# A second buffer for the conditioning sums of a two-layer streaming encoder, with their transposes and VectorE's collection of them at later steps

## The chip, the cores and the metric

The kernel runs on one core of one Trainium2 chip. The metric is device time in microseconds, the median over several executions.

## What is computed

Two layers of an encoder are run for 320 tokens (256 of a prompt, 64 of running streams) of width 1024, all in 32-bit floats. Each layer takes a conditioning vector per token group and turns it into nine vectors of 1024 (a shift, a scale and a gate for each of three parts of the layer); the parts are a feed-forward, a token mixer (retention and differential attention) and a second feed-forward:

```python
mod = (jax.nn.silu(c) @ w_ada[l] + b_ada[l]).reshape(B, N_SUB, 3, D_MODEL)[:, :, :, None, :]
x = x + 0.5 * mod[:, 0, 2] * _swiglu(pre(x, 0), w_ff_up[l, 0], w_ff_down[l, 0])
mix, k_new, v_new, s_new = _token_mix(pre(x, 1), pos, lambda_init, w_in[l], w_out[l], ...)
x = x + mod[:, 1, 2] * mix
x = x + 0.5 * mod[:, 2, 2] * _swiglu(pre(x, 2), w_ff_up[l, 1], w_ff_down[l, 1])
```

Here pre(t, i) is the root-mean-square norm with the i-th scale and shift. The matrix w_ada of a layer is 1024 by 9216; the product with it is what the change is about.

## The kernel before, in words

**Steps.** A layer is 76 steps, each with its own piece of weights: 22 up steps of the first feed-forward (one block of 128 of the 2816 hidden columns, gate and value halves), 8 down steps, 12 of the input projection, 4 of the output projection, and again 22 up and 8 down steps. A step is numbered s in its layer; within a feed-forward f, i counts up steps 0 to 21 and m down steps 0 to 7, and the prediction counts the down steps on as 22 to 29. SyncE (SP) loads a step's weights into one of two buffers (raw, L368 to L379), two steps ahead. ScalarE (ACT) rounds them to a high part (w_hi, its split, L909), VectorE (DVE) and, for a part of the columns, GpSimd (POOL) subtract that from the weights to get the low part (w_lo, L1126 and L1564). TensorE (PE) then multiplies in three passes, high by high, low by high and high by low (L513 to L515): 48 matmuls in an up step, 66 in a down step, each in two halves. Before each half it waits for the half's low part (half_ready, L517). The split of step s + 2 on ScalarE waits for the end of step s on TensorE (step_done), since both use one buffer.

**Around a step on VectorE.** In its instruction order (ffn, L1214) step i is: units of the conditioning sums (ada_unit, L1129), then for an up step the product of gate and value (gate_up, L1188, which waits for ScalarE's silu of the step), for a down step the update of x (down_evac, L1207, which waits for the step's end), then the split of step i + 2.

**The conditioning sums.** w_ada is cut into blocks of 512 columns, 18 to a layer. The first layer's blocks 0 to 5 are made ahead of the loop over layers; the rest, and the next layer's first six, are spread over the feed-forwards by a plan written by hand (ada_plan, L300). It gives (block, place) pairs, where a place counts the blocks in the order in which a layer makes them. A block is four units; SyncE brings a unit (512 KB) to one of four buffers ada_raw behind the weights of a step (load_ada, L393), once VectorE has used that buffer. A unit is four instructions of 128x512 on VectorE (L1137, L1139): each row of the unit times its value of silu(c), for two token groups, added to the sums ada_acc. In the up steps there is one unit in each step and a block takes four steps; from up step 20 on there are two units in each step and a block takes two. In the first feed-forward sums are made in all 30 steps, the last of them after the norm that follows; in the first layer's second feed-forward in steps 0 to 25, in the second layer's in steps 0 to 7.

**Turn and reduction.** ada_acc then holds a partial sum for each of 128 partitions. When the fourth unit is done VectorE drains and says acc_ready (L1144). TensorE transposes the eight 128x128 pieces into two banks of PSUM (turn_acc, L528; the transposes are L533), between the two halves of a step: of the step after the block's last unit (4, 8, 12, 16, 20, and then the down steps 22, 24, 26, 28). VectorE waits for acc_turned and reduces each bank over the partitions into mod (ada_reduce, L1148; L1151), two instructions, right behind the split at the end of the block's last step, so that the wait is for the turn in the step that TensorE does next. The next block's first unit follows and overwrites ada_acc. Place 9 is turned in the second step of the input projection (L835). finish_mod (L1154) adds the bias and the ones when a part's blocks are there.

**Loops.** VectorE and SyncE run the up steps in loops of four steps and down steps 0 to 3 in a loop of two; TensorE has a loop over up steps 12 to 19. Semaphore values and column indices in them are worked out from the loop's register. All engines run the two layers in a loop too. ScalarE and POOL have loops of their own.

Of the kernel before, what the change touches and what calls it, by code (L numbers as in the profile page):

```python
# [19 lines left out]
F32 = mybir.dt.float32  # L20
# [5 lines left out]
P = 128  # L26
# [3 lines left out]
DEPTH = 2  # L30
# [96 lines left out]
def encoder(nc, x_prompt, x_sample, cache_k, cache_v, state_ret, c_prompt, c_sample, w_ada, b_ada, g_norm,  # L127
# [18 lines left out]
    with ExitStack() as ctx:  # L146
# [45 lines left out]
        ada_acc = nc.alloc_sbuf_tensor_at("ada_acc", [P, 2, 512], F32, offset=after_g + 4 * 4096)  # L192
# [47 lines left out]
        acc_turned = sem("acc_turned")  # L240
        first_landed = [sem(f"first_landed{s}") for s in range(2)]
# [118 lines left out]
        def _(sp):  # L360
# [39 lines left out]
            def load_ffn(l, f, s0):  # L400

                bodies, last_up, downs = ada_plan(f)
                for (b, place), n0, n in ((bodies[0], 0, 2), (bodies[1], 2, 3)):
                    with sp.Fori(0, n) as j:
                        for v in range(4):
                            load_up(l, f, s0 + 2 + 4 * n0 + v, 2 + 4 * n0 + v + 4 * j, 2 * j)
                            with if_next(sp, l, b):
                                load_ada(l, b, place, v, j)

                def next_layer(v):  # L410
                    with sp.If(l < DEPTH - 1):
                        load(l, STEPS + v, 0, up_parts(DEPTH - 1, 0, v))

                def pair(block, load_next):
                    for v in range(2):
                        load_next(v)
                        if block:
                            with if_next(sp, l, block[0]):
                                load_ada(l, *block, 2 * v)
                                load_ada(l, *block, 2 * v + 1)  # L420

                pair(last_up, lambda v: load_down(l, f, s0 + UP + v, v, 0))
                with sp.Fori(0, 2) as j:
                    for v in range(2):
                        load_down(l, f, s0 + UP + 2 + v, 2 + v + 2 * j, j)
                        with if_next(sp, l, downs[0][0]):
                            load_ada(l, *downs[0], 2 * v, j)
                            load_ada(l, *downs[0], 2 * v + 1, j)
# [1242 lines left out]
```

## Time and profile before

| | |
|---|---|
| time, median of 3 | 1645.44 us (1642.21 to 1646.52) |
| profiled execution | span 1643.2 us from its first to its last instruction; no other time of it is given |
| granted TensorE clock, mean | 0.937 of full speed |
| TensorE / VectorE / ScalarE / POOL busy | 1469.8 / 1202.0 / 606.7 / 502.7 us |
| read from memory | 255 MB, 159 GB/s over the span |

Busy time counts an engine's instructions without waits, branches and semaphores. In the rows, "idle before" is how long the engine stood still just before an instruction, and the arrow names what ended that; DVEq is VectorE's sequencer, and "issue" is time in which the engine waited for nothing that the profile shows. Times in rows of a timeline are microseconds from the start of the span.

### The profile page before, as it was taken

Reading aid. Unit: us, or ns where it says so; the run is one execution under the profiler, and the core shown is the slowest. Engines: PE = TensorE matmul, PEld = TensorE weight load, DVE = VectorE, ACT = ScalarE, POOL = GpSimd, SP = SyncE. Lnnn points to the kernel's source line nnn. Section 1 sums busy time; section 2 is a strip of 40 time slices with the busy share of each in tenths; the row PEclk is TensorE's granted clock in tenths of the full one; section 3 lists DMA queues with packets and bytes.
Section 4 is the critical chain, followed back from the end, with each engine's and each line's share of the span. In section 5 each row is a group of like instructions: output and inputs, shape, how many; then the busy total and the mean of one; then the engine's idle time right before and its main releaser. Section 6 shows DMA issues by size and latency. Waiting matters only on the chain.

```text
span 1643.2 us, 27178 instructions
## 1 busy us (share of the span) xinstructions
PE 1469.8 (89%) x8865; PEld 1319.9 (80%) x8865; DVE 1202.0 (73%) x1697; ACT 606.7 (37%) x999; POOL 502.7 (31%) x343
## 2 busy tenths in 40 slices
PE   6889998889986889998898999889899769999998
PEld 2589988867763879998887999888677448899998
DVE  3988899987555488889948888998764546874552
ACT  2344432223434344443223444322234333444522
POOL 1134343314001133334323434432330102343432
PEclk9999999999985899999998999989999669999999
DMA  9657777533520147678643777865242204565652
GB/s 311 197 174 211 230 225 217 174 108 124 175 91 7 55 131 214 194 215 231 183 138 95 210 212 213 241 184 188 103 160 92 72 1 129 146 179 145 174 147 63
DMA packets 340962, 261.20 MB, mean 159 GB/s; under 512 B 7968, under 2 KB 288112, under 8 KB 340720
## 3 DMA queue, kind: packets, MB, share of 16 engines
q1 hardware_dynamic: 339456, 255.25, 51.6%
q0 software_dynamic: 1392, 4.46, 0.9%
q8 instruction: 69, 1.13, 0.3%
q14 instruction: 45, 0.37, 0.1%
HBM read 255.22 MB, written 4.46 MB: 158 GB/s over the span
## 4 chain that ended last, share of the span: by engine, by line
PE 47%; DVE 21%; DVEq 13%; DMA 7%; issue 6%; ACT 4%; SPq 1%; ACTq 0%; POOL 0%
PE ps L513 10%; PE ps L514 10%; PE ps L515 10%; DVE ada_acc L1139 9%; DMA ada_raw<-in_w_ada 6%; DVEq L1142 5%; DVEq L1144 4%; PE ps L672 4%; PE ps L677 4%; PE ps L673 4%; DVE w_lo L1126 3%; DVE f_buf L1182 2%; PE ps L533 1%; PE ps L812 1%; DMA first_ada<-in_w_ada 1%
## 5 line engine op out<-in xcount | busy, mean ns | idle before, releaser
L1126 DVE TENSOR_TENSOR w_lo<-raw,w_hi 128x1024 fp32r<-128x1024 f32 (+3 forms) x304 | 429.8, 1455 | 109.5 <-ACT w_hi L909 83.8
L513 PE MATMUL ps<-h_hi,w_hi 128*128 128x320 f32 x1408 | 441.2, 313 | 13.0 <-DVE w_lo L1126 10.3
L514 PE MATMUL ps<-h_lo,w_hi 128*128 128x320 f32 x1408 | 438.3, 311 | 0.0
L515 PE MATMUL ps<-h_hi,w_lo 128*128 128x320 f32 x1408 | 438.3, 311 | 0.0
L909 ACT ACTIVATE w_hi<-raw 128x1024 fp32r<-128x1024 f32 (+1 forms) x304 | 324.9, 1119 | 281.2 <-PE ps L515 188.4
L1139 DVE SCALAR_TENSOR_TENSOR ada_acc<-ada_raw,silu_c,ada_acc 128x512 f32<-128x512 f32 x448 | 391.3, 914 | 34.9 <-DMA ada_raw<-in_w_ada 22.3
L1564 POOL TENSOR_TENSOR w_lo<-raw,w_hi 128x512 fp32r<-128x512 f32 (+1 forms) x112 | 225.1, 2010 | 464.1 <-ACT w_hi L909 464.1
L513 PEld LDWEIGHTS ps<-h_hi,w_hi 128*128 128x128 f32 x1408 | 267.5, 190 | 16.2 <-DVE w_lo L1126 12.9
L514 PEld LDWEIGHTS ps<-h_lo,w_hi 128*128 128x128 f32 x1408 | 267.3, 190 | 0.0
L515 PEld LDWEIGHTS ps<-h_hi,w_lo 128*128 128x128 f32 x1408 | 267.2, 190 | 0.0
L513 PE MATMUL ps<-g_hi,w_hi 128*128 128x320 f32 x704 | 227.3, 323 | 13.4 <-DVE w_lo L1126 13.2
L514 PE MATMUL ps<-g_lo,w_hi 128*128 128x320 f32 x704 | 224.8, 319 | 0.0
L515 PE MATMUL ps<-g_hi,w_lo 128*128 128x320 f32 x704 | 224.4, 319 | 0.0
L513 PEld LDWEIGHTS ps<-g_hi,w_hi 128*128 128x128 f32 x704 | 139.2, 198 | 15.2 <-issue 13.7
L1569 POOL TENSOR_TENSOR g_lo<-f_buf,g_hi 128x320 f32 (+1 forms) x88 | 125.1, 1422 | 81.9 <-ACT g_hi L939 81.9
L514 PEld LDWEIGHTS ps<-g_lo,w_hi 128*128 128x128 f32 x704 | 139.2, 198 | 0.0
L515 PEld LDWEIGHTS ps<-g_hi,w_lo 128*128 128x128 f32 x704 | 138.8, 197 | 0.0
L672 PE MATMUL ps<-w_hi,h_hi 128*128 128x512 f32 (+1 forms) x288 | 118.2, 410 | 4.8 <-ACT h_hi L934 4.8
L1598 POOL TENSOR_TENSOR small<-small,minus_half 128x8 f32<-128x8 f32 (+3 forms) x24 | 31.7, 1325 | 281.3 <-DVE small L1272 281.3
L673 PE MATMUL ps<-w_lo,h_hi 128*128 128x512 f32 (+1 forms) x288 | 113.8, 395 | 0.0
L950 ACT ACT_TABLE_LOAD x40 | 51.3, 1283 | 120.5 <-PE ps L515 115.7
L1555 POOL TENSOR_TENSOR h_lo<-f_buf,h_hi 128x320 fp32r<-128x320 f32 x48 | 43.9, 915 | 162.6 <-ACT h_hi L934 162.6
(156 smaller groups left out, 1602.5 us busy)
## 6 DMA issues: line engine op xcount, KB each, us to landing
raw<-in_w_ff_up SPq DMA_DIRECT2D x176, 512.0 KB, 5.0
ada_raw<-in_w_ada SPq DMA_DIRECT2D x128, 512.0 KB, 6.1
raw<-in_w_ff_down SPq DMA_DIRECT2D x64, 704.0 KB, 6.1
raw<-in_w_in SPq DMA_DIRECT2D x48, 512.0 KB, 4.6
first_ada<-in_w_ada SPq DMA_DIRECT2D x8, 1024.0 KB, 7.1
raw<-in_w_out SPq DMA_DIRECT2D x16, 512.0 KB, 5.5
out<-arena POOLq DMA_DIRECT2D x9, 256.0 KB, 4.1
arena<-in_cache_k SPq DMA_DIRECT2D x2, 1024.0 KB, 5.5
```

What stands on the lines that cost most here:

```text
L513: pe.matmul(out, hi, mhi, start=start, stop=False)
L514: pe.matmul(out, hi, mlo, start=False, stop=False)
L515: return pe.matmul(out, lo, mhi, start=False, stop=stop)
L672: pe.matmul(out, h_hi[:, k, tok], wh, start=(k == 0), stop=False)
L673: pe.matmul(out, h_hi[:, k, tok], wl, start=False, stop=False)
L677: mm = pe.matmul(out, h_lo[:, k, tok], wh, start=False, stop=(k == KB - 1))
L909: act.activation(w_hi[s % 2][:, hf * w:(hf + 1) * w], raw[s % 2][:, hf * w:(hf + 1) * w], ACT.Copy).then_inc(hi_ready, 1)
L1126: dve.tensor_tensor(w_lo[s % 2][:, cols], raw[s % 2][:, cols], w_hi[s % 2][:, cols], ALU.subtract)\
L1139: last = dve.scalar_tensor_tensor(ada_acc[:, g, :], ada_raw[u][:, kk, :], c, ada_acc[:, g, :], ALU.mult, ALU.add)
L1142: dve.drain()
L1564: pool.tensor_tensor(w_lo[s % 2][:, cols], raw[s % 2][:, cols], w_hi[s % 2][:, cols], ALU.subtract)\
L1569: pool.tensor_tensor(block_of(g_lo, i + 2 * j), f_buf[:, i % 2, :], block_of(g_hi, i + 2 * j), ALU.subtract)\
```

## The change

The sums have two buffers, used in turn by even and odd places; the second lies where first_rows is, which is used before the loop over layers alone. The hand-written plan is replaced by a list of blocks with their first step and number of steps. The transposes of a block come in step first + n + 1, one step later on TensorE than before (5, 9, 13, 17, 21 and then 23, 25, 27, 29), and its reduction behind the split in the same step on VectorE, two steps later in VectorE's order than before. A semaphore mod_read, raised by the reduction, is waited for before the next block is turned, since the two PSUM banks are still one set. finish_mod(64, 72) moves from after up step 7 to after up step 10. Units, transfers and what they wait for are in the same steps as before. Loops over steps are written out on SyncE, TensorE and VectorE; place 9 is turned and reduced where it was.

```diff
-        ada_acc = nc.alloc_sbuf_tensor_at("ada_acc", [P, 2, 512], F32, offset=after_g + 4 * 4096)
+        ada_acc = [nc.alloc_sbuf_tensor_at(f"ada_acc{s}", [P, 2, 512], F32, offset=after_g + (4 + s) * 4096) for s in range(2)]
...
+        mod_read = sem("mod_read")
...
-        def ada_plan(f):
+        def ada_blocks(f):
             if f == 0:
-                return [(6, 0), (8, 2)], (11, 5), [(12, 6), (13, 7), (14, 8), (15, 9)]
-            return [(16, 10), (0, 12)], (3, 15), [(4, 16), (5, 17), None, None]
+                return [(6 + p, p, 4 * p, 4) for p in range(5)] + [(11 + p, 5 + p, UP - 2 + 2 * p, 2) for p in range(5)]
+            return [(16, 10, 0, 4), (17, 11, 4, 4), (0, 12, 8, 4), (1, 13, 12, 4), (2, 14, 16, 4),
+                    (3, 15, 20, 2), (4, 16, 22, 2), (5, 17, 24, 2)]
+
+        def units_in(f, step):
+            for b, place, first, n in ada_blocks(f):
+                if first <= step < first + n:
+                    each = 4 // n
+                    return b, place, range(each * (step - first), each * (step - first + 1))
+            return None
+
+        def turned_in(f, step):
+            for b, place, first, n in ada_blocks(f):
+                if first + n + 1 == step:
+                    return b, place
+            return None
+
+        def acc_of(place):
+            return ada_acc[place % 2 if place >= 0 else 0]
...
+                for q in range(2, UP + DOWN + 2):
+                    if q < UP:
+                        load_up(l, f, s0 + q, q, 0)
+                    elif q < UP + DOWN:
+                        load_down(l, f, s0 + q, q - UP, 0)
+                    elif f == 0:
+                        load_in(l, q - UP - DOWN)
+                    else:
+                        with sp.If(l < DEPTH - 1):
+                            load(l, STEPS + q - UP - DOWN, 0, up_parts(DEPTH - 1, 0, q - UP - DOWN))
+                    if (units := units_in(f, q - 2)) is not None:
+                        b, place, us = units
+                        with if_next(sp, l, b):
+                            for u in us:
+                                load_ada(l, b, place, u)
...
             def turn_acc(l, place, j=0):
                 pe.wait_ge(acc_ready, ADA_AHEAD + l * ADA_BLOCKS + place + j + 1)
+                if place >= 0:
+                    pe.wait_ge(mod_read, ADA_AHEAD + l * ADA_BLOCKS + place + j)
...
-                for v in range(2, 8):
-                    up_step(l, s0 + v, 0, (lambda: turn_next(bodies[0])) if v == 4 else None)
-                for v in range(4):
-                    up_step(l, s0 + 8 + v, 0, (lambda: turn_next(bodies[0], 1)) if v == 0 else None)
-                with pe.Fori(0, 2) as j:
-                    for v in range(4):
-                        up_step(l, s0 + 12 + v, 2 * j, (lambda: turn_next(bodies[1], j)) if v == 0 else None)
-                for v in (UP - 2, UP - 1):
-                    up_step(l, s0 + v, 0, (lambda: turn_next(bodies[1], 2)) if v == UP - 2 else None)
+                for v in range(2, UP):
+                    up_step(l, s0 + v, 0, lambda: turn_late(v))
                 d0 = s0 + UP
                 for m in range(KB):
-                    last = last_up if m == 0 else downs[m // 2 - 1]
-                    down_step(l, d0 + m, 0, f, m == 0, (lambda: turn_next(last)) if m % 2 == 0 else None)
+                    down_step(l, d0 + m, 0, f, m == 0, lambda: turn_late(UP + m))
...
             def ada_reduce(l, b, place, j=0):
                 dve.wait_ge(acc_turned, ADA_AHEAD + l * ADA_BLOCKS + place + j + 1)
                 for g in range(2):
-                    dve.tensor_reduce(mod[:, g, bass.ds((b + j) * 4, 4)],
-                                      ps[:, 4 + g, :].rearrange("p (c k) -> p c k", c=4), AX.X, ALU.add)
+                    last = dve.tensor_reduce(mod[:, g, bass.ds((b + j) * 4, 4)],
+                                             ps[:, 4 + g, :].rearrange("p (c k) -> p c k", c=4), AX.X, ALU.add)
+                last.then_inc(mod_read, 1)
...
+                for i in range(UP):
+                    ada(i)
                     gate_up(l, s0 + i, 0, f, i)
                     split(l, s0 + i + 2)
-                reduce(last_up)
...
+                    reduce(i)
+                    if f == 1 and i == 10:
+                        finish_mod(64, 72)
+                for m in range(KB):
+                    ada(UP + m)
                     down_evac(l, f, m)
                     if f == 0 and m == 5:
                         finish_mod(24, 48)
                     if m < 7:
                         with dve.If(l < DEPTH - 1) if f == 1 and m == 6 else nullcontext():
                             split(l, s0 + UP + m + 2)
-                    if m == 5:
-                        reduce(block)
+                    reduce(UP + m)
```

## Rows read from the trace of the kernel before

**Rows 1.** The page: span, and busy time of each engine.
```profile
span 1643.2 us, 27178 instructions
PE 1469.8 (89%) x8865; PEld 1319.9 (80%) x8865; DVE 1202.0 (73%) x1697; ACT 606.7 (37%) x999; POOL 502.7 (31%) x343
```

**Rows 2.** Groups by line: busy us, mean ns | idle before, releaser.
```profile
L1151 DVE TENSOR_REDUCE mod<-ps 128x512 f32 (+1 forms) x64 | 40.8, 677 | 10.8 <-PE ps L533 10.8
```

**Rows 3.** Waits of TensorE, whole span: us in total, times, longest.
```profile
PE ps L533 <- DVEq L1144: 49.7, 21, 4.3
...
PE ps L513 <- DVE w_lo L1126: 23.6, 11, 4.5
```

**Rows 4.** Timeline of TensorE, place 9: start, us, operation [idle before].
```profile
366.20 0.55 PE L533 MATMUL ps<-tab,ada_acc 128*128 128x128 f32 x3 [3.87 <-DVEq L1144]
```

**Rows 5.** Windows: length, busy PE, PEld, DVE, ACT, POOL, PEclk, DMA, GB/s.
```profile
229.00:340.00 111.00, 94.21 (x609) 92.38 (x608) 102.80 (x122) 29.48 (x31) 37.52 (x15) 0.95 0.66 201
...
1465.00:1550.00 85.00, 85.00 (x582) 85.00 (x581) 41.66 (x38) 40.56 (x56) 32.03 (x24) 1.00 0.59 161
```

**Rows 6.** Waits of VectorE in 107 to 229.
```profile
DVE f_buf L1193 <- ACT t_buf L950: 2.5, 4, 1.2
```

**Rows 7.** Waits of VectorE in 619 to 750; all others listed are issue.
```profile
DVE ada_acc L1139 <- DMA ada_raw<-in_w_ada: 5.5, 6, 1.6
```

**Rows 8.** Window of step 4, first layer's first feed-forward.
```profile
100.33:112.92 12.59, 9.67 (x59) 9.40 (x57) 9.81 (x13) 2.92 (x4) 3.17 (x3) 0.86 0.54 165
```

**Rows 9.** Timeline of TensorE: the turn in that step.
```profile
106.93 1.09 PE L533 MATMUL ps<-tab,ada_acc 128*128 128x128 f32 x8 [2.92 <-DVEq L1144]
```

**Rows 10.** Timeline of VectorE, 107 to 116.
```profile
107.87 2.50 DVE L1126 TENSOR_TENSOR w_lo<-raw,w_hi 128x1024 fp32r<-128x1024 f32 x2 [0.21 <-issue]
110.30 1.27 DVE L1151 TENSOR_REDUCE mod<-ps 128x512 f32 x2
...
115.04 0.49 DVE L1193 TENSOR_TENSOR f_buf<-ps,t_buf 128x320 f32<-128x320 f32 x1 [1.18 <-ACT t_buf L950]
```

**Rows 11.** Timeline of VectorE: the sums of step 6, second feed-forward.
```profile
642.87 2.90 DVE L1139 SCALAR_TENSOR_TENSOR ada_acc<-ada_raw,silu_c,ada_acc 128x512 f32<-128x512 f32 x4 [1.28 <-DMA ada_raw<-in_w_ada]
```

**Rows 12.** Timeline of VectorE at the end of the first feed-forward.
```profile
340.53 0.67 DVE L1203 SCALAR_TENSOR_TENSOR x<-ps,mod,x 128x256 f32<-128x256 f32 x2 [0.16 <-PE ps L515]
344.22 2.15 DVE L1174 RECIPROCAL rstd<-std 128x320 f32<-128x320 f32 x1 [3.01 <-ACT std L931]
```

**Rows 13.** Timeline of ScalarE in the second feed-forward's down steps.
```profile
786.33 2.65 ACT L909 ACTIVATE w_hi<-raw 128x1408 fp32r<-128x1408 f32 x2 [1.30 <-PE ps L515]
...
803.67 2.65 ACT L909 ACTIVATE w_hi<-raw 128x1408 fp32r<-128x1408 f32 x2 [7.06 <-PE ps L515]
...
827.84 2.65 ACT L909 ACTIVATE w_hi<-raw 128x1408 fp32r<-128x1408 f32 x2 [5.82 <-PE ps L515]
...
837.52 2.65 ACT L909 ACTIVATE w_hi<-raw 128x1408 fp32r<-128x1408 f32 x2 [6.67 <-PE ps L515]
```

**Rows 14.** Timeline of VectorE in the same down steps.
```profile
796.16 2.50 DVE L1126 TENSOR_TENSOR w_lo<-raw,w_hi 128x1408 fp32r<-128x1408 f32 x2 [0.24 <-issue]
...
806.57 5.15 DVE L1126 TENSOR_TENSOR w_lo<-raw,w_hi 128x1408 fp32r<-128x1408 f32 x2 [0.31 <-ACT w_hi L909]
...
820.67 0.68 DVE L1203 SCALAR_TENSOR_TENSOR x<-ps,mod,x 128x256 f32 x2 [0.44 <-issue]
821.55 2.50 DVE L1126 TENSOR_TENSOR w_lo<-raw,w_hi 128x1408 fp32r<-128x1408 f32 x2 [0.21 <-issue]
...
829.26 1.62 DVE L1126 TENSOR_TENSOR w_lo<-raw,w_hi 128x1408 fp32r<-128x1408 f32 x1 [0.74 <-ACT w_hi L909]
```

**Rows 15.** Timeline of TensorE: the first turn of the second layer.
```profile
912.59 0.66 PE L533 MATMUL ps<-tab,ada_acc 128*128 128x128 f32 x4 [1.33 <-DVEq L1144]
```

**Rows 16.** Waits of TensorE, 1405 to 1640.
```profile
PE ps L533 <- DVEq L1144: 2.2, 2, 1.3
```

**Rows 17.** Timeline of VectorE: an update in straight code.
```profile
309.35 0.67 DVE L1203 SCALAR_TENSOR_TENSOR x<-ps,mod,x 128x256 f32<-128x256 f32 x2 [0.18 <-issue]
```

More of the change, by code:

```diff
@@ L400, in load_ffn @@
             def load_ffn(l, f, s0):
-                bodies, last_up, downs = ada_plan(f)
-                for (b, place), n0, n in ((bodies[0], 0, 2), (bodies[1], 2, 3)):
-                    with sp.Fori(0, n) as j:
-                        for v in range(4):
[L406 to L428, printed above, removed]
-                pair(downs[2], lambda v: load_down(l, f, s0 + UP + 6 + v, 6 + v, 0))
-                pair(downs[3], (lambda v: load_in(l, v)) if f == 0 else next_layer)
+                for q in range(2, UP + DOWN + 2):
[13 more added lines that the diff above has]
+                                load_ada(l, b, place, u)
             def load_in(l, i):
@@ L1214, in ffn @@
             def ffn(l, f, s0):
-                bodies, last_up, downs = ada_plan(f)
-                def ada(block, units, j=0):
-                    if block:
-                        with if_next(dve, l, block[0]):
-                            for u in units:
-                                ada_unit(l, block[1], u, j)
-                def reduce(block, j=0):
-                    if block:
-                        with if_next(dve, l, block[0]):
-                            ada_reduce(l, *block, j)
@@ L1228, in ffn @@
-                for block, n0, n in ((bodies[0], 0, 2), (bodies[1], 2, 3)):
-                    with dve.Fori(0, n) as j:
-                        for v in range(4):
-                            i = 4 * n0 + v
-                            ada(block, (v,), j)
-                            gate_up(l, s0 + i, 2 * j, f, i)
-                            split(l, s0 + i + 2, 2 * j)
-                        reduce(block, j)
-                    if f == 1 and n0 == 0:
-                        finish_mod(64, 72)
@@ L1238, in ffn, with ada, reduce @@
-                for i in (UP - 2, UP - 1):
-                    ada(last_up, (2 * (i % 2), 2 * (i % 2) + 1))
+                def ada(step):
+                    if (units := units_in(f, step)) is not None:
+                        b, place, us = units
+                        with if_next(dve, l, b):
+                            for u in us:
+                                if (place, u) != (9, 3):
+                                    ada_unit(l, place, u)
+                def reduce(step):
+                    if (block := turned_in(f, step)) is not None:
+                        with if_next(dve, l, block[0]):
+                            ada_reduce(l, *block)
```

32 lines of the change are left out of this document (10 added, 22 removed).

## Prediction, made before the change was run

> **What bounds the kernel now.** The page and the list of lines come first: TensorE (PE) is busy 89% of a span of 1643.2 us, VectorE (DVE) 73% [rows 1]. VectorE's largest groups are the splits of the weights and the sums of the conditioning; the 64 reductions, most of which the change moves, take 40.8 us, 0.68 each, 1.27 a pair, and only 10.8 us of waiting for a turn stands before them, all in the opening [rows 2]. Next the waits of TensorE: the transposes of the sums wait 49.7 us in 21 places for the drain that announces a finished sum, and the weight matmuls 23.6 us for VectorE's splits [rows 3]. So the wait that the change aims at is real. Two of the 21, 3.87 us each, belong to place 9, which stays where it is (one in each layer) [rows 4]: 42 us are in play, if nothing else holds TensorE there.
>
> The windows by stretch say what else. Where no sums are made (1465 to 1550) TensorE runs without a gap, 582 matmuls in 85.0 us, 146 ns each: 7.04 us for an up step of 48, 9.68 for a down step of 66. In the down stretch (229 to 340) TensorE is busy 94 of 111 us and VectorE 103, the rest being drains and issue [rows 5]. VectorE's waits name the limit: in the first up stretch it waits 2.5 us for ScalarE's silu, so there it has time left; in the up stretch of the second feed-forward (619 to 750) it waits 5.5 us for transfers and never for TensorE or ScalarE [rows 6, 7]. There, and in every down stretch while sums are made, VectorE sets the pace. A turn that waits is then mostly the place where TensorE notices it; the next place is the split that starts the next step.
>
> **The change part by part.** The sum is against the profiled execution; its span of 1643.2 lies 2.2 us under the median of 1645.4, and I carry the difference over.
>
> The turns. In the first layer's first feed-forward the turn in step 4 waits 2.92 us at 106.93, and behind that wait the granted clock falls (0.86 over the step, so part of it at the lower level, 1.2 GHz): the step takes 12.59 us where 7.04 and some 0.9 for the transposes (eight in 1.09, the last beside the next matmul) would do [rows 8, 9]. Walked anew: the second half of step 4 ends near 107.5, but step 5 needs VectorE's split, which starts at 107.87 and has its first half near 109.1 [rows 10]; TensorE waits 1.6 us there. Step 5 with its transposes ends near 117.1 instead of 112.92 + 7.04 = 120.0, so 2.9 us earlier. VectorE gets 2.0 to 2.4 of it: the reduction at 110.30 (1.27) no longer stands there, and it need not wait 1.18 for silu at 115.04 [rows 10]. I take -2.0; bounds 0 and -2.9. From there on TensorE is the bound and the shift carries.
>
> The up stretch from 619. VectorE's own chain sets the pace, so the four turn waits there turn into waits for splits. What can shrink is transfer wait: the reduction now follows the split of step 7 and lies in the 1.28 us wait at 642.87 [rows 11]; others lose such cover. I take -1.0; bounds 0 and -5.5, all transfer waits there [rows 7].
>
> The down stretches. VectorE pays in every step for four or eight sums, an update and a split; the number of reductions between the start of the stretch and the last update is four before and four after, so its chain does not move. In the first feed-forward of both layers VectorE comes to its last update as TensorE ends (the wait at 340.53 is 0.16 us [rows 12]): the turn waits (up to 4.3 us each [rows 3]) become waits for the split at a step's start, and I cost their removal at nothing. The cover is VectorE's chain; without it the 17 us that TensorE idles there (111 less 94 [rows 5]) would be open. In the second feed-forward sums stop after step 25, and here it pays. ScalarE's splits, released by TensorE, mark the step ends: 786.33, 803.67, 827.84, 837.52 [rows 13]. Walked anew with VectorE's times kept: step 24, without a turn, ends at 796.0; step 25 starts on the split at 796.16 + 1.62 = 797.8 and with transposes (1.09) ends at 808.6; step 26 starts when the first half of the split at 806.57 is done (a whole of 5.15, so near 810.8) and ends at 820.5; step 27 starts at 821.55 + 1.62 = 823.2 and ends at 834.0 (the first half of a split takes 1.62 us, as at 829.26) [rows 14]. That is -3.5 against 837.52, after which TensorE is alone; bounds 0 and -4.5.
>
> The second layer. The turn at 912.59 waits 1.33 us and the one near 1428 1.28 (its stretch has 2.2 in two places) [rows 15, 16]. By the same walk the split that follows is done just as TensorE comes: -1.0 and -1.3; bounds 0 and -2.3 together.
>
> The loops. The change also writes out what VectorE, TensorE and SyncE ran in loops. In the loop an update waits 0.42 to 0.44 us for issue (register arithmetic for the index), in the straight code of such a stretch 0.18 [rows 14, 17]: 0.25 for each of four steps and about 0.1 on their splits, 1.1 per feed-forward, in the three whose down stretch VectorE bounds: -3.3; bounds 0 and -5 (a gain of the up steps too). Longer code could cost fetching; no row of forward straight code shows such a stop, bound 0 to +3.
>
> Added waits. TensorE now waits before a turn for the reduction of the block before. Behind that wait stand the second half of the step and its step_done, for which ScalarE's split, VectorE's update and SyncE's buffers wait. That reduction stands on VectorE right behind a split that TensorE's running step needed, half a step (3.5 or 4.8 us) ahead, against 1.27 for the pair: 0; bounds 0 and +1. VectorE's wait for the turn comes after the split of two steps on, which itself needed the end of an earlier step: 0. The order of SyncE's transfers and what each waits for is the same; POOL's queue is untouched, and its timing follows ScalarE. The last reduction of the first feed-forward (block 14) falls behind the last update; the square, the sum and the root before the norm leave VectorE 3.01 us idle and hide its 1.27 [rows 12].
>
> Where POOL's split hits VectorE: the split at 806.57, behind ScalarE's at 803.67 and beside POOL's, takes 5.15 us, the one at 821.55 takes 2.50: 2.65 more [rows 13, 14]. The Trainium skill (SBUF — State Buffer, Who interferes with whom) says that a VectorE instruction with two SBUF inputs contends with a reading GpSimd one, while a reduction never does. By that a reduction moved beneath a POOL split would be free; by the row alone POOL's price stays once per step wherever it falls, which is what the sum takes.
>
> Sum: -2.0 - 1.0 - 3.5 - 1.0 - 1.3 - 3.3 = -12.1 us: 1631.1 of span, 1633.3 in the median.
>
> **The rivals.** (A) The waits only change place: VectorE is the chain in the tail of 786 to 837 too and in the layer starts, and only the written-out loops pay: -3.6, 1641.8. For it: TensorE's 23.6 us of waits for splits [rows 3] would grow by what the turns lose. Against: the tail has no sums. 0.20.
> (B) More than the forecast: TensorE ends steps earlier, so ScalarE's and POOL's splits come earlier (after a step end at 796.0 ScalarE's 2.65 us bring POOL to 798.7, where the split begun at 796.16 ends and the reduction begins [rows 13, 14]). If six of the eleven down reductions cover 1.2 us of a POOL split, 7 us more: 1626. The Trainium skill's rule above is what would make it so. 0.10.
> (C) The turn waits go wholly, 42 us, because VectorE was held by them: 1603. Against it, VectorE waits for no turn after the opening [rows 2] and never for TensorE in 619 to 750 [rows 7]. 0.03.
> (D) Slower. A reduction used to stand before the short unit of a block (two of its four sums are plain products), in the step that TensorE's transposes lengthen; now it stands before a longer one (2.90 us at 642.87 [rows 11]). Where VectorE's lead over TensorE at a step's start falls below 1.27, each of the 17 moved reductions in up steps costs up to 1.27: +21.6, with the gains above 1655. After the first turn I give VectorE 2.0 to 2.4 us of lead, so transfers must come a microsecond later than now. 0.09.
> (E) The change does not do what it says: the buffer is unused and nothing moves; excluded by the diff, 0.
>
> **How the numbers follow.** Forecast 0.58: 1633.3, by its bounds 1628 to 1639. A 0.20, B 0.10, C 0.03, D 0.09. The range reaches over A and B and leaves out C and D (0.12): 1625 to 1645. A measurement of this kernel tells about 0.3% (4.9 us) from no change: 1640.5. Faster takes forecast, B, C and nothing of A: 0.70; same takes A and the edges: 0.21; slower 0.09.
>
> **What would show it.** Right: turns hardly wait (42 us to under 5), waits for splits grow from 23.6 to 45 or so, TensorE's step 27 of the first layer's second feed-forward starts on a split, the update waits 0.2 us for issue everywhere, VectorE's idle time in 619 to 750 hardly changes. Wrong: if waits for splits do not grow while the turns stop waiting, C holds; if transfers' share of VectorE's waits grows above 22 us and up steps take over 7.3 us each, D; if sums of 3.45 us become rarer, B.

## The result, and the profile after

The changed kernel takes **1654.65 us** (median of 4 runs, 1653.40 to 1656.02) beside 1644.39 for the kernel before on the same chip: a ratio of 1.0059, 95% interval [1.0040, 1.0077]. Timed again later beside the experiments it gave 1.0058 [1.0042, 1.0075]. It is slower by about 10 us, which is small (0.6%) but clear of noise, where 12 us of gain were forecast; it lies outside the predicted range.

The page of the changed kernel: span, busy time, and the chain of work that ended last by engine. The first two lines answer to [rows 1].

```profile
span 1652.5 us, 26882 instructions
PE 1472.9 (89%) x8865; PEld 1313.8 (80%) x8865; DVE 1213.7 (73%) x1697; ACT 608.4 (37%) x999; POOL 498.1 (30%) x343
...
PE 35%; DVE 26%; DVEq 16%; DMA 11%; issue 7%; ACT 4%; SPq 2%; ACTq 0%; POOL 0%
```

The same chain in the kernel before:

```profile
PE 47%; DVE 21%; DVEq 13%; DMA 7%; issue 6%; ACT 4%; SPq 1%; ACTq 0%; POOL 0%
```

TensorE's share of the chain has fallen from 47% to 35%; VectorE and its sequencer (34% to 42%) and transfers (7% to 11%) have taken most of its place. VectorE is also busy 11.7 us longer with the same 1697 instructions. Waits of TensorE in the changed kernel, against [rows 3]:

```profile
PE ps L518 <- DVE w_lo L1123: 70.5, 44, 7.1
...
PE ps L540 <- DVEq L1141: 7.8, 2, 3.9
```

The turns (now L540) wait in the two places of place 9 alone, so the wait that the change aims at is gone, all 42 us of it. Waits for VectorE's splits have grown from 23.6 to 70.5 us, by more than that. VectorE's groups in the changed kernel, and the same groups before (busy, mean ns | idle before):

```profile
L1123 DVE TENSOR_TENSOR w_lo<-raw,w_hi 128x1024 fp32r<-128x1024 f32 (+3 forms) x304 | 410.8, 1392 | 106.0 <-ACT w_hi L906 80.8 <-issue 24.7
L1136 DVE SCALAR_TENSOR_TENSOR ada_acc<-ada_raw,silu_c,ada_acc 128x512 f32<-128x512 f32 x448 | 409.2, 954 | 40.2 <-DMA ada_raw<-in_w_ada 27.4 <-issue 0.6
L1148 DVE TENSOR_REDUCE mod<-ps 128x4 f32<-128x512 f32 x64 | 40.9, 677 | 13.9 <-PE ps L540 13.6
L1134 DVE TENSOR_SCALAR ada_acc<-ada_raw,silu_c 128x512 f32<-128x512 f32 x64 | 39.8, 662 | 25.6 <-DMA ada_raw<-in_w_ada 25.0 <-issue 0.6
```

```profile
L1126 DVE TENSOR_TENSOR w_lo<-raw,w_hi 128x1024 fp32r<-128x1024 f32 (+3 forms) x304 | 429.8, 1455 | 109.5 <-ACT w_hi L909 83.8 <-issue 25.3
L1139 DVE SCALAR_TENSOR_TENSOR ada_acc<-ada_raw,silu_c,ada_acc 128x512 f32<-128x512 f32 x448 | 391.3, 914 | 34.9 <-DMA ada_raw<-in_w_ada 22.3
...
L1137 DVE TENSOR_SCALAR ada_acc<-ada_raw,silu_c 128x512 f32<-128x512 f32 x64 | 27.9, 475 | 14.8 <-DMA ada_raw<-in_w_ada 13.4 <-issue 1.4
```

Splits got 19.0 us cheaper, sums 17.9 and plain products 11.9 us dearer: more of POOL's work now runs beside the sums and less beside the splits (in the three up stretches of the table below 67.3 us beside sums against 36.7 before, and 88.5 beside splits against 109.7). Waits for the units' transfers grew from 35.7 us (22.3 + 13.4) to 52.4, and 16.1 of these 16.7 us lie in the three up stretches.

**Where it went.** VectorE's timeline gives marks that do not depend on how far TensorE runs ahead: the ends of its product in steps 2 and 20 and of its update in step 29 of a feed-forward. "Up" is step 2 to 20 and "down" step 20 to 29, for the first layer's two feed-forwards and the second layer's first (where sums are made); "rest" is all else. In us, from the profiled execution of each kernel (experiments below):

| kernel | opening | up | down | rest | span |
|---|---|---|---|---|---|
| before | 98.2 | 140.0, 142.7, 139.6 | 103.0, 98.0, 103.0 | 818.7 | 1643.2 |
| changed | 100.2 | 144.9, 146.1, 147.2 | 101.8, 93.2, 102.1 | 817.0 | 1652.5 |
| changed, again | 98.7 | 147.1, 145.0, 148.8 | 101.9, 94.8, 101.9 | 816.6 | 1654.8 |
| e1 old steps | 99.8 | 139.2, 138.2, 142.2 | 103.1, 96.7, 102.1 | 819.7 | 1641.0 |
| e2 early turn | 100.9 | 141.7, 143.6, 147.8 | 116.1, 107.9, 115.6 | 818.5 | 1692.1 |
| e3 POOL late | 102.7 | 145.0, 143.9, 146.2 | 105.9, 96.9, 105.9 | 813.5 | 1660.0 |
| e4 units first | 99.0 | 134.8, 135.7, 133.6 | 101.9, 94.8, 101.9 | 811.6 | 1613.3 |
| e5 reduction later | 99.8 | 145.5, 142.6, 147.8 | 102.1, 93.2, 101.9 | 814.7 | 1647.6 |
| e6 TensorE held | 98.7 | 145.1, 145.5, 145.1 | 99.5, 96.2, 98.7 | 817.3 | 1646.1 |
| e7 old steps, units first | 98.6 | 136.7, 135.5, 135.9 | 103.0, 96.8, 101.4 | 817.9 | 1625.8 |
| e8 e5 and e6 in one | 99.4 | 139.8, 136.5, 142.4 | 102.3, 96.9, 100.8 | 820.2 | 1638.3 |
| e10 e4, TensorE held | 98.6 | 134.9, 136.7, 134.9 | 102.3, 96.8, 98.0 | 819.7 | 1621.9 |

The down stretches give 6.9 us, about as forecast. The three up stretches lose 15.9, where -4.0 was forecast for them: 19.9 of the 21.4 us between the forecast span and the measured one. So the question is what happens in up steps.

In windows of the first up stretch (length, busy PE, PEld, DVE, ACT, POOL, PEclk, DMA, GB/s) the kernel before comes first, the changed one second, e4 third. TensorE ran without a gap in the kernel before, and does not in the changed one:

```profile
107.00:229.00 122.00, 122.00 (x832) 121.97 (x833) 106.81 (x125) 54.68 (x73) 48.48 (x33) 0.99 0.72 214
```

```profile
107.00:229.00 122.00, 117.02 (x794) 115.02 (x793) 105.59 (x122) 55.14 (x72) 47.56 (x33) 1.00 0.68 203
```

```profile
107.00:229.00 122.00, 122.00 (x842) 121.97 (x841) 111.17 (x129) 56.77 (x75) 48.98 (x33) 1.00 0.76 228
```

**How an up step hangs together.** VectorE's timeline in the changed kernel, one block of four units (first sums at 172.94):

```profile
170.52 2.50 DVE L1123 TENSOR_TENSOR w_lo<-raw,w_hi 128x1024 fp32r<-128x1024 f32 x2 [0.56 <-issue]
172.94 0.87 DVE L1134 TENSOR_SCALAR ada_acc<-ada_raw,silu_c 128x512 f32<-128x512 f32 x2
173.89 1.41 DVE L1136 SCALAR_TENSOR_TENSOR ada_acc<-ada_raw,silu_c,ada_acc 128x512 f32<-128x512 f32 x2
...
176.26 2.70 DVE L1123 TENSOR_TENSOR w_lo<-raw,w_hi 128x1024 fp32r<-128x1024 f32 x2 [0.23 <-issue]
181.71 3.78 DVE L1136 SCALAR_TENSOR_TENSOR ada_acc<-ada_raw,silu_c,ada_acc 128x512 f32<-128x512 f32 x4 [2.75 <-DMA ada_raw<-in_w_ada]
...
186.42 2.50 DVE L1123 TENSOR_TENSOR w_lo<-raw,w_hi 128x1024 fp32r<-128x1024 f32 x2 [0.21 <-issue]
188.84 1.27 DVE L1148 TENSOR_REDUCE mod<-ps 128x4 f32<-128x512 f32 x2
190.04 3.77 DVE L1136 SCALAR_TENSOR_TENSOR ada_acc<-ada_raw,silu_c,ada_acc 128x512 f32<-128x512 f32 x4
```

SyncE's queue at the same time:

```profile
173.26 1.00 SPq L397 DMA_DIRECT2D raw<-in_w_ff_up  x2
174.50 0.94 SPq L416 DMA_DIRECT2D ada_raw<-in_w_ada  x1
```

The unit used at 181.71 was issued at 174.50, behind the up weights, whose slot came free only when the split of 170.52 had ended. VectorE could use it 7.2 us after its issue. In the meantime VectorE had only the cheap unit (two of its four sums are plain products, 2.3 us) and the next split to do: it stood still for 2.75 us. This is a ring: a split ends, SyncE issues the unit some 1.5 us later, the unit lands about 6 us after that, and behind its sums, in VectorE's order, stands the next split but one, whose end starts the ring again. Before, the 1.27 us reduction stood just ahead of the cheap unit, in the step that has the least work. After, it stands ahead of the block's third unit. The same up step by the place of its unit in the block (means over the 51 up steps 3 to 19, from the timelines of VectorE and SyncE; the step's length between the ends of two splits; in brackets the wait for the unit's transfer):

| kernel | 1st unit | 2nd | 3rd | 4th | block | waits | sums and splits | landing |
|---|---|---|---|---|---|---|---|---|
| before | 7.80 (.08) | 7.23 (.19) | 7.22 (.34) | 7.60 (.59) | 29.85 | 1.20 | 23.15 | 5.87 |
| changed | 6.68 (.46) | 8.23 (1.25) | 8.43 (.11) | 7.73 (.44) | 31.07 | 2.26 | 23.88 | 6.25 |
| e1 | 7.57 (.00) | 7.38 (.15) | 7.16 (.32) | 7.49 (.51) | 29.60 | 0.98 | 23.52 | 5.97 |
| e5 | 7.62 (.10) | 7.79 (.47) | 7.30 (.36) | 8.08 (.79) | 30.79 | 1.72 | 24.52 | 6.21 |
| e6 | 6.78 (.11) | 8.39 (1.14) | 8.26 (.01) | 7.68 (.49) | 31.11 | 1.75 | 23.96 | 6.12 |
| e8 | 7.47 (.13) | 7.54 (.35) | 7.00 (.24) | 7.65 (.68) | 29.66 | 1.40 | 23.46 | 5.98 |
| e4 | 6.48 (.00) | 7.15 (.00) | 8.05 (.00) | 7.28 (.08) | 28.96 | 0.08 | 23.86 | 6.13 |
| e7 | 7.48 (.00) | 7.40 (.00) | 6.70 (.00) | 7.37 (.09) | 28.95 | 0.09 | 23.98 | 6.05 |

Against before, a block of four takes 1.22 us more: 1.06 of waits for units and 0.73 of longer sums and splits, less 0.57 that other waits (ScalarE, issue) gave back. The brackets and sums depend by up to 0.15 on how short gaps and overlaps are counted. The 54 up steps of the other table are 13.5 such blocks, 16.5 us; it shows 15.9, and 18.6 in the second profile.

### The profile page after: what moved, and what is told of

Its sections match the earlier page's. It is cut to its first block, busy times and chain, and to the rows that moved or that the text cites. A ratio compares the mean times of both kernels' runs of the same rounds, so it can differ in the third digit from the quotient of the medians.

```text
span 1652.5 us, 26882 instructions
## 1 busy us (share of the span) xinstructions
PE 1472.9 (89%) x8865; PEld 1313.8 (80%) x8865; DVE 1213.7 (73%) x1697; ACT 608.4 (37%) x999; POOL 498.1 (30%) x343
## 3 DMA queue, kind: packets, MB, share of 16 engines
q0 software_dynamic: 1392, 4.46, 0.8%
## 4 chain that ended last, share of the span: by engine, by line
PE 35%; DVE 26%; DVEq 16%; DMA 11%; issue 7%; ACT 4%; SPq 2%; ACTq 0%; POOL 0%
DVE ada_acc L1136 11%; DMA ada_raw<-in_w_ada 10%; DVEq L1139 6%; PE ps L518 6%; DVEq L1141 6%; PE ps L520 6%; PE ps L519 6%; PE ps L669 4%; DVE w_lo L1123 4%; PE ps L670 4%; PE ps L674 4%; DVE f_buf L1180 2%; DVE ada_acc L1134 2%; DVE f_buf L1191 1%; PE ps L809 1%
## 5 line engine op out<-in xcount | busy, mean ns | idle before, releaser
L1123 DVE TENSOR_TENSOR w_lo<-raw,w_hi 128x1024 fp32r<-128x1024 f32 (+3 forms) x304 | 410.8, 1392 | 106.0 <-ACT w_hi L906 80.8
L1136 DVE SCALAR_TENSOR_TENSOR ada_acc<-ada_raw,silu_c,ada_acc 128x512 f32<-128x512 f32 x448 | 409.2, 954 | 40.2 <-DMA ada_raw<-in_w_ada 27.4
L1544 POOL TENSOR_TENSOR w_lo<-raw,w_hi 128x512 fp32r<-128x512 f32 (+1 forms) x112 | 218.6, 1951 | 349.5 <-ACT w_hi L906 349.5
L936 ACT ACTIVATE g_hi<-f_buf 128x320 f32 (+1 forms) x88 | 41.3, 469 | 240.6 <-DVE f_buf L1191 240.6
```

Of the source, the lines that this page charges most:

```text
L1123: dve.tensor_tensor(w_lo[s % 2][:, cols], raw[s % 2][:, cols], w_hi[s % 2][:, cols], ALU.subtract)\
L1136: last = dve.scalar_tensor_tensor(acc_of(place)[:, g, :], ada_raw[u][:, kk, :], c, acc_of(place)[:, g, :], ALU.mult, ALU.add)
L1544: pool.tensor_tensor(w_lo[s % 2][:, cols], raw[s % 2][:, cols], w_hi[s % 2][:, cols], ALU.subtract)\
```

## The experiments

**e1, e2, e3, e4** ran on one chip, beside the kernel before at 1644.58 us.

e1 puts transposes and reductions back at the old steps and keeps the second buffer and the written-out loops (the first pair of lines is TensorE's, the second VectorE's; due_in returns the block whose first + n + its last argument is the step):

```diff
-                    if (block := turned_in(f, step)) is not None:
+                    if (block := due_in(f, step, 0)) is not None:
...
-                    if (block := turned_in(f, step)) is not None:
+                    if (block := due_in(f, step, -1)) is not None:
```

> The changed kernel with the transposes and the reductions back at their old steps; two buffers, the added wait and the written-out loops stay. Three theories for the loss of some 10 us. (1) Relative pace: no longer held at the turn, TensorE runs further ahead of VectorE, so POOL's split of the weights is released earlier and falls on VectorE's sums (3.34 to 3.58 us a unit in the up steps after, 2.99 to 3.20 before) and not beside VectorE's own split; and sums wait longer for their unit. (2) The place of the reduction in VectorE's order alone costs it. (3) The written-out loops (code loading, other issue times) or the second buffer cost it. By (1) and (2) this runs at 1641 to 1646 us, as before or a little under (cheaper issue); by (3) at 1652 to 1656.

Measured: 1640.07 us, 0.9971 [0.9950, 0.9992]. The turns wait 44.8 us in 20 places again, and the kernel is faster than either. So the loss, some 14 us against this run, is the placement's, and what else the change does (buffer, written-out loops) is a small gain.

e2 takes the first of the two edits alone: transposes at the old steps, reductions two steps late.

> The changed kernel with the transposes alone back at their old steps; the reductions stay two steps late. By (1), TensorE is held again where the sum is late, so units take about 3.0 us again in the up steps and the time is 1642 to 1647 us; by (2) and (3) it stays at 1652 to 1656. In between would mean that both (1) and (2) have a share.

Measured: 1693.96 us, 1.0293 [1.0265, 1.0321], far worse than expected. TensorE's waits:

```profile
PE ps L547 <- DVE mod L1155: 58.4, 11, 7.2
PE ps L547 <- DVEq L1148: 31.1, 20, 3.9
```

Here the new semaphore binds. With blocks of two steps in the down half, a turn at the old step needs the reduction of the block before, which is two steps late and so not done: 58.4 us in 11 places, and the down stretches take 13, 10 and 13 us more. With the transposes late as well the same wait never appears in TensorE's list: the two moves belong together.

Its up steps, where this wait never occurs, say more than its time. A block takes 30.91 us there (7.28, 7.65, 8.31, 7.67), against 29.60 in e1 and 31.07 in the changed kernel, though units are waited for about as little as in e1. The reduction is gone from the first step, but that step is only 0.29 us shorter than in e1: VectorE waits in it 0.92 us a step for ScalarE's silu (0.27 in e1). The third step is 1.15 us longer. So the late reduction costs 1.3 us a block with the transposes at their old steps too, and what swallows the saving need not be a transfer.

e3 lets POOL start its split only after VectorE's update of the step:

```diff
+                        pool.wait_ge(gf_ready, l * 2 * FB + f * FB + u + 2 * j + 3)
                         split(l, s0 + u + 2, j)
...
+                    pool.wait_ge(x_ready, (l * 3 + 2 * f) * KB + m + 1)
                     split(l, s0 + UP + m + 2)
```

> The changed kernel with one wait more on POOL: its split of step i+2 waits until VectorE has finished the product (or the update) of step i, so that it runs beside VectorE's own split and not on the sums. By (1), units go to 3.0 us or under and splits from 2.58 up to 2.8: some 0.2 us a step over 51 up steps, 1642 to 1648 us, with the wait for units left as it is; if POOL comes late for TensorE's second half, some of that is lost. By (2) and (3) no change, 1652 to 1657.

Measured: 1660.54 us, 1.0086 [1.0059, 1.0112], above what either side expected. VectorE's two largest groups:

```profile
L1123 DVE TENSOR_TENSOR w_lo<-raw,w_hi 128x1024 fp32r<-128x1024 f32 (+3 forms) x304 | 512.7, 1727 | 104.6 <-ACT w_hi L906 79.5 <-issue 24.7
L1136 DVE SCALAR_TENSOR_TENSOR ada_acc<-ada_raw,silu_c,ada_acc 128x512 f32<-128x512 f32 x448 | 326.8, 770 | 42.5 <-DMA ada_raw<-in_w_ada 29.7 <-issue 0.6
```

The sums are freed (770 ns against 954), and the splits pay more than that (1727 against 1392). Delaying POOL is no cure: it moves the meeting to the splits, and that is dearer. What the meeting on the sums costs by itself this run does not tell.

e4 has SyncE issue a step's units before it waits for the slot of the up weights, one step earlier. Everything else is the changed kernel:

```diff
                 for q in range(2, UP + DOWN + 2):
+                    if q > 2:
+                        load_units(q)
                     if q < UP:
                         load_up(l, f, s0 + q, q, 0)
...
-                    if (units := units_in(f, q - 2)) is not None:
...
+                    if q == 2:
+                        load_units(q)
```

> The changed kernel with SyncE issuing a step's unit of w_ada before it waits for the buffer of the weights of that step, one step earlier than now. In the changed kernel VectorE waits 0.51 to 0.61 us a step of the 51 up steps for units (0.28 to 0.39 before). If that wait is what VectorE's pace hangs on, it goes to near 0 and the time falls by 0.5 x 51 = 25 us at most, to 1630 to 1640 us, as far as TensorE lets it. If the units are late because of the traffic itself and not the order, less than 5 us comes back.

Measured: 1615.75 us, 0.9819 [0.9788, 0.9849], 29 us under the kernel before and some 39 under the changed one. That is more than the 25 us that the expectation gave as the most: of 39.2 us in the profiled executions 34.1 lie in the three up stretches and 5.4 in "rest". The chain of work that ended last:

```profile
PE 51%; DVE 23%; DVEq 16%; issue 5%; ACT 4%; DMA 1%; ACTq 0%; SPq 0%; POOL 0%
```

Transfers fall from 11% of the chain to 1%, VectorE's waits for units from 52.4 us to 18.7 (11.3 of them once, in the opening), and a block takes 28.96 us. In the changed kernel SyncE waited for a unit's own buffer only 4.1 us in all, behind the wait for the weights' slot; in e4 it waits 126.7 us for these buffers, in 46 places, and issues each unit as its buffer comes free. The first step is still short (6.48) and the third long (8.05), but nothing is waited for any more, so their sum is what counts.

**e5, e6, e7** ran together, beside the kernel before at 1642.32. They ask whether the late place costs by the reduction (theory R) or by TensorE's freedom (theory T).

e5 moves the reduction; the last four-step block (first step 16) keeps its place:

```diff
+        def reduced_in(f, step):
+            for b, place, first, n in ada_blocks(f):
+                if first + n + (3 if first < 16 else 1) == step:
+                    return b, place
+            return None
...
-                    if (block := turned_in(f, step)) is not None:
+                    if (block := reduced_in(f, step)) is not None:
...
-                    if f == 1 and i == 10:
+                    if f == 1 and i == 12:
```

> Edit: the changed kernel, TensorE's transposes where the change puts them, but VectorE's reduction of each four-step conditioning block two more steps later, so that it stands again ahead of the first unit of a block, as before the change, and no longer ahead of the third. The changed kernel stood at 1.0059 of the kernel before (about 1654 us), the kernel with both at the old places at 0.9971 (1640 us). Theory R (the reduction's place counts: ahead of a block's first unit it filled the wait for that unit's transfer, ahead of the third it fills nothing, and the first unit is now waited for): this edit gives the loss back, 1638 to 1646 us, and VectorE's wait for the first unit's transfer in the up steps falls from about 0.55 us per step to about 0.3. Theory T (TensorE, no longer held by its transposes at the old places, runs its steps at another distance to VectorE and SyncE, and the transfers land later or collide more): the reductions' place is nothing, 1651 to 1657 us, and the landing time stays at 6.2 us against 5.9 before. A value between, 1647 to 1650, would give each a part.

Measured: 1647.40 us, 1.0020 [1.0002, 1.0038]. Some 40% of the way to e1 came back, between the two theories. The steps are even again and the second unit's wait falls from 1.25 to 0.47 us, but sums and splits rise to 24.5 us a block and the up stretches hardly shorten.

e6:

```diff
+                    for b, place, first, n in ada_blocks(f):
+                        if place != 9 and first + n == step:
+                            with if_next(pe, l, b):
+                                pe.wait_ge(acc_ready, ADA_AHEAD + l * ADA_BLOCKS + place + 1)
```

> Edit: the changed kernel, both transposes and reductions at their late places, but TensorE waits at the old step for the block's sums all the same (the wait alone is put back, the transposes stay two steps later). Theory T (TensorE's freedom at the old place is what does the harm): the hold brings back the old distances, 1638 to 1646 us. Theory R (the reduction's place does): the hold frees nothing on VectorE and adds TensorE waits where it is not the one that is late; the up steps stay at 7.7 to 7.8 us each, and the down steps lose the 4 us a half that the change had given, so 1652 to 1668 us.

Measured: 1647.26 us, 1.0028 [1.0004, 1.0052]. Again between them, a third of the way to e1, though its interval reaches into the changed kernel's. The second unit is still waited for (1.14 us), and a block takes as long as in the changed kernel (31.11 against 31.07). The down stretches of the first feed-forwards are shorter (101.8 to 99.5, 102.1 to 98.7), the one of the second is longer (93.2 to 96.2). Neither theory stands alone.

e7 is e1 with e4's edit.

> Edit: second buffer and written-out loops kept, transposes and reductions at the old steps, and SyncE issues a step's unit of conditioning weights before it waits for the slot of the step's up weights, one step earlier, as in the run that stood at 0.9819 of the kernel before (1615.75 us) with the late places. It asks what the late places are worth once no unit is waited for. Theory R (the late place costs through the wait for the first unit's transfer alone, and is otherwise the gain forecast: TensorE no longer held): with that wait gone the late places pay, so this kernel is slower than 0.9819, 1622 to 1630 us. Theory T, and any theory by which the late place costs through something else than the transfers: the old places stay better by the 14 us that they were better by, 1598 to 1606 us. Equal, 1612 to 1619: both the harm and the gain of the late places run through the same transfers.

Measured: 1625.66 us, 0.9894 [0.9869, 0.9919]. Without a transfer to wait for the late places beat the old ones, 0.9819 against 0.9894, where with it they lose, 1.0059 against 0.9971. The sign of the placement hangs on the ring, as R had it. But a block is as long in both (28.96 and 28.95), and in both TensorE stands idle less than 1 us in a whole up stretch: this is TensorE's own time for a block, four steps of 7.04 and the transposes. VectorE has some 0.7 us a block to spare there, in which it waits for ScalarE, so the pair does not tell whether the late place costs through transfers alone; e4's lead is in the down stretches, the last steps of the up ones and in "rest", which I have not taken apart.

**e8, e9, e10** ran together, beside the kernel before at 1643.29. e8 holds the edits of e5 and e6 at once, so only the transposes are late and the rest as of old.

> Edit: the two edits before this in one: VectorE's reduction of a four-step block stands again ahead of a block's first unit (two more steps later), and TensorE waits at the old step for the block's sums, so that only the transposes themselves are two steps late. Each edit alone gave about half of the loss back (1.0020 and 1.0028, against 1.0059 for the change and 0.9971 for the old places), and in their profiled executions neither shortened the up stretches (about 160 us each, against 154 to 157 for the old places). Theory U (the up steps need both: the reduction in the step whose first unit is the cheap one, so that VectorE's steps are even and the next transfer has time to land, and TensorE at its old distance, so that GpSimd's parts fall on the split less often together with the sums): up stretches of 153 to 157 us, down stretches of 83 to 86, so 1630 to 1638 us. Theory M (it is the place of the transposes on TensorE that stretches the up steps, by when they pass the block on to VectorE, or the two parts do not add): up stretches of 159 to 162, 1642 to 1650 us.

Measured: 1633.21 us, 0.9938 [0.9913, 0.9963] (12 runs, 1621 to 1642). Theory U by its time. (The expectation cuts its stretches elsewhere than the table.) In the table the up stretches are back at 139.8, 136.5 and 142.4, where e1 has 139.2, 138.2 and 142.2, a block at 29.66. VectorE's timeline of the first two units of a block:

```profile
138.73 3.04 DVE L1134 TENSOR_TENSOR w_lo<-raw,w_hi 128x1024 fp32r<-128x1024 f32 x2 [0.21 <-issue]
141.69 1.28 DVE L1159 TENSOR_REDUCE mod<-ps 128x4 f32<-128x512 f32 x2
142.89 0.87 DVE L1145 TENSOR_SCALAR ada_acc<-ada_raw,silu_c 128x512 f32<-128x512 f32 x2
143.84 1.42 DVE L1147 SCALAR_TENSOR_TENSOR ada_acc<-ada_raw,silu_c,ada_acc 128x512 f32<-128x512 f32 x2
...
146.22 2.93 DVE L1134 TENSOR_TENSOR w_lo<-raw,w_hi 128x1024 fp32r<-128x1024 f32 x2 [0.23 <-issue]
149.28 3.30 DVE L1147 SCALAR_TENSOR_TENSOR ada_acc<-ada_raw,silu_c,ada_acc 128x512 f32<-128x512 f32 x4
```

The reduction fills the cheap step and the second unit is there when it is wanted. e5 and e6 each save 0.3 to 0.4% and the two together 1.2%: in the up steps they only work together, a block of 30.79 or 31.11 alone and 29.66 with both. What the hold adds to e5 is 1.06 us a block of shorter sums and splits, 0.32 of waits, and transfers that land in 5.98 us rather than 6.21.

e9 is the changed kernel once more.

> The changed kernel itself once more, unedited, beside the others on one chip. All theories: 1.004 to 1.0077 of the kernel before, as it had been in four runs, so about 1649 to 1657 us, and the waits of its up steps as in its first profile (the second unit of a block waited for by over 1 us, steps of 6.7, 8.2, 8.4 and 7.7 us).

Measured: 1654.56 us, 1.0058 [1.0042, 1.0075], with steps of 6.4, 8.6, 8.4 and 7.7 us and 1.40 us of wait for the second unit: the pattern is the kernel's own, not one execution's.

e10 is e4 with e6's hold.

> Edit: late places, units issued one step earlier ahead of the wait for the weights' slot (the run that stood at 0.9819), and TensorE held at the old step until the block's sums are there. The hold alone, on the changed kernel, shortened the down stretches of the first halves from 86.1 to 84.1 us and left the up stretches as they were. Theory H (what the hold gives in the down steps is VectorE's sums with less of GpSimd beside them, 6.71 against 7.89 us a step, and it needs no transfer): 1607 to 1614 us. Theory N (with no unit waited for, every TensorE wait put back is lost): the up stretches go from 149.5 to 151 or more, 1617 to 1627 us.

Measured: 1619.79 us, 0.9842 [0.9813, 0.9870], outside theory H's range and inside N's, and not told apart from e4 by its interval. The up stretches are 2.4 us longer than e4's in all. The third down stretch shortens to 98.0 us and "rest" grows. e4 stays the best of what was tried.

## Why the prediction was wrong

**The turns at the start: right by itself, wrong in what follows.** I had step 5 end 2.9 us earlier and start on the split with 1.6 us of wait. In the changed kernel it starts at 111.06, 1.35 us after TensorE is ready, and step 6 starts at 119.09; with step 2 starting 2.2 us later than before (88.07 against 85.83), that is 3.1 earlier. The step that failed is the sentence behind it, "From there on TensorE is the bound and the shift carries". TensorE was the bound in the kernel before (122.00 of 122.00 us busy from 107 to 229), and in the changed one it is not (117.02). VectorE stopped at once for its next unit:

```profile
119.65 2.90 DVE L1136 SCALAR_TENSOR_TENSOR ada_acc<-ada_raw,silu_c,ada_acc 128x512 f32<-128x512 f32 x4 [1.57 <-DMA ada_raw<-in_w_ada]
```

VectorE had little to spare: in 107 to 229 it waited 2.7 us for units and 3.9 for ScalarE before, and 7.4 for units and none for ScalarE after. I counted its wait for silu [rows 6] as time left over and did not walk from a unit's use back to its issue; the sum has longer waits for units at nothing, and they grew by 16.7 us.

**The up stretch of the second feed-forward: -1.0 forecast, +3.4 measured.** The text says that the reduction now covers the wait at 642.87 [rows 11] and that "others lose such cover". The others weighed more. The cover lost was in the step with the cheap unit. Nor did I price the shortened step: less work there lets nothing come earlier, as a unit lands some 7.7 us after the split that releases it (1.5 to its issue, 6.2 to its landing) whatever VectorE does.

**The second layer: -1.0 forecast for its first turn, +7.6 measured in its first up stretch,** for the same reason. The last turn had -1.3: cut by the same marks, the up stretch it stands in went from 127.0 to 126.8 us. The 1.7 us that "rest" lost lie between the two feed-forwards of the second layer (276.2 to 274.5), where nothing was forecast.

**The down stretches: right in size.** -3.5 for the tail and -1.1 for the written-out loops made -4.6 in the second feed-forward; its down stretch shortened by 4.8, and by 3.2 in the second profile. e1, with the loops written out and the turns at their old steps, has 1.3 of it. In the first feed-forwards -1.1 each was forecast, for the loops alone, and -1.2 and -0.9 measured; e1 has +0.1 and -0.9, so that the loops made the first of these is not shown. The update there waits 0.18 to 0.21 us for issue, as forecast:

```profile
816.82 0.68 DVE L1201 SCALAR_TENSOR_TENSOR x<-ps,mod,x 128x256 f32<-128x256 f32 x2 [0.18 <-issue]
```

**Added waits: right.** mod_read shows in no list of the changed kernel's waits. e2 shows what it costs where the order of the moves is not kept.

**POOL's price: wrong in the up steps.** "POOL's price stays once per step wherever it falls" was the sum's term; VectorE's three groups above pay 10.8 us more (17.9 + 11.9 - 19.0). In the down stretches the term holds: sums and plain products cost 9.5 us more there, splits 9.5 less, and all of the 11.9 us of plain products are there, five instructions of 2.8 us beside a POOL split. In the up stretches sums and plain products cost 17.9 more and splits 8.2 less, so 9.7 us are paid on top. Held back, TensorE lets POOL fall on the splits (e8: VectorE busy 1200.9 us, e5: 1218.8). But that alone does not bring the price down: in e6 and e4 POOL meets the sums as little as before (37.4 and 31.9 us in the up stretches), and sums and splits cost 23.96 and 23.86 us a block, as in the changed kernel. What makes this price was not isolated.

**The rivals.** A's mark came true, waits for splits growing by all that the turns lose, but they grew beyond it. B gained nothing: of the 64 reductions ten touch any POOL instruction. C fell. The side was D's. It named the right place (the reduction no longer before the short unit but before a longer one, transfers later), and the third step does take 1.21 us more. Its condition was another: it asked whether VectorE's lead over TensorE falls below 1.27 us, and what decides is that the emptied step gives nothing back (its saving goes into waits for units, 0.46 and 1.25 us, or for ScalarE in e2); a part is POOL's. Its marks could not have told: the kernel before had up steps of 7.46 us on the mean, over 7.3, and 22.3 us of waits for transfers ahead of sums, over 22. It had 0.09; the waits for transfers in [rows 7] deserved a walk of their own and would have given it more.

What stays open: what makes POOL's price in the up steps, why units land 0.2 to 0.4 us later when TensorE is free (6.2 against 5.9 to 6.0 us), and how the 1.2% of e8 divides between waits and POOL, since each changes the other.

## What to carry to other kernels

When an engine in a ring with a transfer gets its work shifted between steps, sum the ring (use, release, issue, landing, use) and compare it with each step's own work: here work taken out of the lightest step saved next to nothing (0.3 us of 1.27 in e2, 0.1 us over two steps in the changed kernel), and added to a heavier one it cost nearly in full (1.15 and 1.21 us). A wait for another engine that disappears from the list pays only as far as the next thing on the path has slack; look for that next thing in the waits of the engine that sets the pace. Where a queue issues in order, a transfer whose own buffer comes free first is late for nothing behind one that waits for its slot: moving it ahead took the changed kernel from 1.0059 to 0.9819 of the kernel before (e4), some 39 us.

## What the runs showed of the hardware

A plain product with a single tensor input was stretched by POOL: the pair at 284.77 takes 3.26 us where two take 0.87 otherwise, beside POOL's split.

```profile
283.57 1.27 DVE L1148 TENSOR_REDUCE mod<-ps 128x4 f32<-128x512 f32 x2
284.77 3.26 DVE L1134 TENSOR_SCALAR ada_acc<-ada_raw,silu_c 128x512 f32<-128x512 f32 x2
```

```profile
284.38 2.97 POOL L1544 TENSOR_TENSOR w_lo<-raw,w_hi 128x1280 fp32r<-128x1280 f32 x1 [0.88 <-ACT w_hi L906]
```

The reduction in front of it, whose end lies beside the same split, keeps its 1.27. By the Trainium skill (SBUF — State Buffer, Who interferes with whom) a plain product can run in a mode that uses both pairs of ports and then blocks against GpSimd, while a reduction never contends; both agree with these rows.
